# Gate rows, residual rows and split operands moved inside the product stages of a three-layer diffusion transformer

## Chip, cores and metric

One core of a Trainium2 chip. The metric is the device time of one launch in microseconds. All arithmetic is fp32; large products are made of fp32r parts (see below).

## The reference, cut to what matters

Width 1024, 512 latent tokens (`x`) and 256 context tokens (`ctx`). A first block (pooling, differential attention and a bidirectional RWKV scan, merged, then a routed expert layer) works on the latent rows alone. Two further layers work on both: one with hyena and mLSTM mixers, one with latent attention, each with a convolutional FFN (inner width 2816). Every residual step has the same form:

```
mod   = silu(c) @ w_ada + b_ada                    # six chunks of 1024, one is the gate of this step
x     = x + gate * (mixed @ w_out)                 # gate: one value a column, the same for all tokens
...
return rmsnorm(x, final_norm)                      # x * rsqrt(mean(x*x) + 1e-6) * final_norm
```

There are six such steps: output projection and experts in the first block, output projection and FFN down in each of the two layers; those of the middle layer also update `ctx`, with gates of its own. All but the experts' step go through `project_add`, five calls.

## The kernel before, in words

The program is a line of stages. `stage` (L46 to L66) opens a block in which each engine runs its own list; at its end all engines meet, and GpSimd clears the stage's semaphores. Work of one stage never overlaps work of the next, except for one weight tile that is asked for at the end of a product stage (`bring_ahead`) and lands behind the barrier.

`products` (L169) is the stage that does all large products. Weights of 256 columns come by DMA from SyncE (SP) into a landing buffer of 8 KB a partition. With `split=True`, ScalarE copies the landed tile into a leading part rounded to fp32r, in two halves (L276), VectorE subtracts to get the rest (L284), and TensorE adds three products, rest times leading, leading times rest, leading times leading (L340). The next step's load waits until the present tile is parted. Operands must lie in two parts as well. Results go from PSUM through `evac`, on ScalarE or VectorE. `side` are small products for later modulations, woven between. `pooled` is work for GpSimd in the same block. Without `split` (the branch products, `w_br`) three weight slots are filled from the stage's start on, and no weight is brought ahead.

`modulation_tiles` leave each modulation in `m.mod` with the column on the partitions. The residual step needs it along the free axis, the same on all 128 partitions. `gate_rows` (L444) makes that in a stage of its own: VectorE spreads a chunk to 128 equal columns (`wide`, L463), TensorE multiplies with the identity (L457, eight matmuls a row), VectorE copies from PSUM (L466). `halves` (L107) is another stage that splits the whole operand (L115 ScalarE, L121 VectorE). `project_add` (L1808) then runs the products with an evacuation of two instructions a tile: times the gate (L1821), added to the row (L1822). The order at the end of the first block is: gates' products, branch products, `load` of x (L825, a stage with one DMA and a wait), `gate_rows`, `halves`, `project_add`. The second block begins with a `load` of ctx. The FFN of the middle layer splits its operand inside the product stage, per k (`whole=`), so it has no `halves`, and nor has the last layer, whose FFN up writes both parts.

The end: `load` of the final gain, `head_norms` (L615 on: square, sum, root, reciprocal, times root, times gain, each VectorE pass over 128x4096), and a stage with one store of 2 MB (L2242).

`normed` (L475) makes row norms ahead of the products: ScalarE squares with a sum (L543) into a scratch tile, then the root (L537).

Of the kernel before, what the change touches and what calls it, by code (L numbers as in the profile page):

```python
# [168 lines left out]
def products(nc, m, jobs, xT, evac, evac_on, banks=4, kt=KD, wslots=WSLOTS, beside=None, width=512, split=False, k_chunks=1, side=(), pooled=None, whole=None):  # L169
# [18 lines left out]
    with ExitStack() as ctx:  # L188
# [8 lines left out]
        with stage(nc, w_landed=wslots, rounded=1, parted=1, made=1, read=1, chain=1, aux=1, side_landed=SIDE_SLOTS, side_made=1, side_copied=1, side_turned=1, side_read=1, spread=1, own_rounded=1, own_parted=1) as (  # L197
# [24 lines left out]
            def _(sp):  # L222
# [4 lines left out]

                ahead = 2 if split else wslots
# [22 lines left out]
                if split and m.ahead_next < len(m.ahead_of):  # L251
                    sp.wait_ge(parted_sem, 2 * len(steps))
                    bring_ahead(m, sp)

# [13 lines left out]
            def round_weights(act, s):  # L268
                if whole is not None and steps[s][0] == 0:
                    round_operands(act, s)  # L270
                if s >= 2:
                    act.wait_ge(made_sem, ends[s - 1])
                act.wait_ge(landed[s % wslots], landed_before[s % wslots] + sum(landings[s % wslots:s + 1:wslots]))
                n = steps[s][2]
                for k0, k1 in k_halves(s):
                    nc.scalar.copy(leading[s % 2][:, k0:k1, 0:n], slots[s % wslots][:, k0:k1, 0:n]).then_inc(rounded_sem, 1)  # L276

            def part_weights(dve, s):
                if whole is not None and steps[s][0] == 0:
                    part_operands(dve, s)  # L280
                n = steps[s][2]
                for q, (k0, k1) in enumerate(k_halves(s)):
                    dve.wait_ge(rounded_sem, 2 * s + q + 1)
                    nc.vector.tensor_tensor(rest[s % 2][:, k0:k1, 0:n], slots[s % wslots][:, k0:k1, 0:n], leading[s % 2][:, k0:k1, 0:n].bitcast(F32), ALU.subtract).then_inc(parted_sem, 1)  # L284

# [23 lines left out]
            def _(pe):  # L309
# [134 lines left out]
def gate_rows(nc, m, ctx, i, chunk, n, more=None):  # L444

    (rows,) = buffers(nc, ctx, gate_rows=[n, D])
    total = n + (more is not None)
    of = [(chunk, j) for j in range(n)] + ([(more[0], 0)] if more else [])
    with ExitStack() as own:
        (wide,) = buffers(nc, own, wide=[total, KD, P])  # L450
        with stage(nc, widened=1, made=1) as (block, widened_sem, made_sem):
            @block.tensor
            def _(pe):
                for j in range(total):
                    pe.wait_ge(widened_sem, j + 1)
                    for f in range(KD):
                        mm = nc.tensor.matmul(m.ps[:, 2 * j + f // 4, (f % 4) * P:(f % 4 + 1) * P], wide[:, j, f, :], m.ident, start=True, stop=True)  # L457
                    mm.then_inc(made_sem, 1)

            @block.vector  # L460
            def _(dve):
                for j, (c, kind) in enumerate(of):
                    nc.vector.tensor_copy(wide[:, j, :, :], bc(m.mod[:, i, KD * c:KD * (c + 1), kind:kind + 1], P)).then_inc(widened_sem, 1)  # L463
                for j in range(n):
                    dve.wait_ge(made_sem, j + 1)
                    nc.vector.tensor_copy(rows[:, j, :], m.ps[:, 2 * j:2 * j + 2, :].rearrange("p a b -> p (a b)"))  # L466
                if more:
                    dve.wait_ge(made_sem, total)
                    for h in range(2):
                        R = slice(64 * h, 64 * (h + 1))  # L470
                        nc.vector.tensor_copy(more[1][R, :], m.ps[R, 2 * n + h, :])
    return rows


def normed(nc, m, tiles, hT, affine, loads=None):  # L475
# [8 lines left out]
    with ExitStack() as ctx:  # L484
        b = Memory()
        b.sq, b.diag, b.whole, b.ss, b.root, b.rstd, b.gain = buffers(nc, ctx, sq=[2, D], diag=[n, P], whole=[4 if parts else 1, 512], ss=[n], root=[n], rstd=[n], gain=[len(kinds), KD])
# [435 lines left out]

# [2065 lines left out]
```

## Time and profile before

| | |
|---|---|
| median of 3 runs | 4127.73 us (4127.23, 4127.73, 4131.23) |
| span of the profiled execution | 4129.6 us; the page gives no time around it |
| TensorE matmul busy | 3568.4 us, 86% |
| VectorE / ScalarE / GpSimd busy | 1697.6 / 908.8 / 31.9 us |
| mean granted TensorE clock | 0.923 |
| DMA | 483.19 MB, 117 GB/s on average |

The span runs from the first to the last instruction. Busy times of different engines overlap and can't be added. The granted clock is 1.0 at 2.4 GHz and 0.5 at 1.2 GHz. The page's chain of waits holds only the last norm and store, since each stage ends at a barrier; to see what a stage costs, one reads the time between first instructions of neighbouring stages.

### The profile page before, as it was taken

How to read it: one execution, taken by the hardware profiler on the slowest of the kernel's cores; microseconds unless marked ns; L12 is line 12 of the kernel's file. 1: busy time of each engine (PE TensorE's matmuls, PEld its weight loads, DVE VectorE, ACT ScalarE, POOL GpSimd, SP SyncE). 2: the span in 40 equal slices, each digit the busy share in tenths (PEclk: the TensorE clock that was granted, in tenths of full speed). 3: DMA queues.
4: the chain of work that ended last, by engine and by line, in shares of the span. 5: the costliest groups of instructions: out<-in, count | busy, mean ns of one | idle time of the engine just before them, and what ended most of it. 6: DMA issues, size and time to landing. Idle time of an engine off the chain costs nothing. (4 is left out here: it accounts for less than half of the span.)

```text
span 4129.6 us, 71104 instructions
## 1 busy us (share of the span) xinstructions
PE 3568.4 (86%) x31286; PEld 2846.9 (69%) x31286; DVE 1697.6 (41%) x2906; ACT 908.8 (22%) x1502; POOL 31.9 (1%) x32
## 2 busy tenths in 40 slices
PE   5979997677997899995989976899989859979996
PEld 3858895655847655654746846888889856568886
DVE  3644544472123211113545256444452353245633
ACT  2135431041202111112011151211121212323221
POOL 0000000000000000000000000000000000000000
PEclk8979997888998899997999988999999989989998
DMA  6130004302344699993521100244422110013322
GB/s 225 57 129 4 4 4 166 123 1 94 92 143 161 253 408 410 412 412 122 174 81 56 52 2 31 65 124 115 121 75 64 43 36 25 1 52 93 97 74 80
DMA packets 274375, 483.19 MB, mean 117 GB/s; under 512 B 11947, under 2 KB 190668, under 8 KB 265397
## 3 DMA queue, kind: packets, MB, share of 16 engines
q1 hardware_dynamic: 267252, 453.97, 31.5%
q0 software_dynamic: 1728, 16.78, 1.1%
q10 hardware_dynamic: 5120, 8.39, 0.6%
q8 instruction: 220, 3.60, 0.4%
q14 instruction: 55, 0.44, 0.0%
HBM read 449.74 MB, written 29.36 MB: 116 GB/s over the span
## 5 line engine op out<-in xcount | busy, mean ns | idle before, releaser
L340 PE MATMUL banks<-leading,w_rest 128*128 128x512 f32 (+2 forms) x1920 | 698.9, 364 | 58.4 <-DVE w_rest L284 58.4
L340 PE MATMUL banks<-rest,w_leading 128*128 128x512 f32 (+2 forms) x1920 | 690.1, 359 | 0.0
L340 PE MATMUL banks<-leading,w_leading 128*128 128x512 f32 (+2 forms) x1920 | 688.9, 359 | 0.0
L284 DVE TENSOR_TENSOR w_rest<-land,w_leading 128x1024 fp32r<-128x1024 f32 (+2 forms) x328 | 306.9, 977 | 433.8 <-ACT w_leading L276 433.8
L276 ACT CAST w_leading<-land 128x1024 fp32r<-128x1024 f32 (+2 forms) x328 | 262.9, 849 | 875.4 <-DMA land<-in_w_in 303.0
L340 PEld LDWEIGHTS banks<-leading,w_rest 128*128 128x128 f32 (+1 forms) x1920 | 363.8, 189 | 128.8 <-DVE w_rest L284 46.0
L340 PE MATMUL banks<-w_rest,leading 128*128 128x256 f32 (+3 forms) x1332 | 394.4, 296 | 56.8 <-DVE w_rest L284 56.8
L340 PEld LDWEIGHTS banks<-leading,w_leading 128*128 128x128 f32 (+1 forms) x1920 | 364.1, 190 | 59.1
L340 PEld LDWEIGHTS banks<-rest,w_leading 128*128 128x128 f32 (+1 forms) x1920 | 364.0, 190 | 56.6
L340 PE MATMUL banks<-w_leading,rest 128*128 128x256 f32 (+3 forms) x1332 | 389.8, 293 | 0.0
L340 PE MATMUL banks<-w_leading,leading 128*128 128x256 f32 (+3 forms) x1332 | 389.4, 292 | 0.0
L340 PEld LDWEIGHTS banks<-w_rest,leading 128*128 128x128 f32 x1332 | 261.6, 196 | 66.3 <-DVE w_rest L284 53.0
L340 PEld LDWEIGHTS banks<-w_leading,rest 128*128 128x128 f32 x1332 | 261.4, 196 | 1.4
L340 PEld LDWEIGHTS banks<-w_leading,leading 128*128 128x128 f32 x1332 | 261.1, 196 | 1.4
L340 PE MATMUL banks<-w_rest,first_up_leading 128*128 128x256 f32 x528 | 150.4, 285 | 8.6 <-DVE w_rest L284 8.6
L340 PE MATMUL banks<-w_leading,first_up_rest 128*128 128x256 f32 x528 | 150.2, 284 | 0.0
L340 PE MATMUL banks<-w_leading,first_up_leading 128*128 128x256 f32 x528 | 150.2, 284 | 0.0
L2041 PE MATMUL banks<-wd,hT 128*64 128x512 f32 x512 | 125.3, 634 | 26.9 <-ACT hT L2065 26.9
L2098 DVE TENSOR_TENSOR y<-banks,expert_gate 128x512 f32<-128x512 f32 x32 | 22.1, 692 | 276.2 <-PE banks L2041 276.2
L2026 PE MATMUL banks<-wg,xT 128*64 128x256 f32 x1024 | 117.6, 383 | 1.2 <-ACT xT L2053 1.2
L1821 DVE TENSOR_TENSOR t<-banks,gate_rows 128x256 f32<-128x256 f32 x96 | 40.6, 423 | 185.6 <-PE banks L340 185.3
L2026 PE MATMUL banks<-wu,xT 128*64 128x256 f32 x1024 | 115.9, 379 | 0.0
(550 smaller groups left out, 5220.5 us busy)
## 6 DMA issues: line engine op xcount, KB each, us to landing
wg<-in_w_exp_gate SPq DMA_DIRECT2D x32, 2048.0 KB, 12.7
wu<-in_w_exp_up SPq DMA_DIRECT2D x32, 2048.0 KB, 14.8
wd<-in_w_exp_down SPq DMA_DIRECT2D x32, 2048.0 KB, 11.9
ws<-in_ada_w SPq DMA_DIRECT2D x96, 512.0 KB, 3.8
land<-in_w_in SPq DMA_DIRECT2D x41, 1024.0 KB, 5.4
land<-in_ffn_up SPq DMA_DIRECT2D x44, 512.0 KB, 5.4
land<-in_ffn_up SPq DMA_DIRECT2D x88, 256.0 KB, 3.3
land<-in_ffn_down SPq DMA_DIRECT2D x24, 768.0 KB, 4.9
```

Source lines behind the costliest of these rows:

```text
L276: nc.scalar.copy(leading[s % 2][:, k0:k1, 0:n], slots[s % wslots][:, k0:k1, 0:n]).then_inc(rounded_sem, 1)
L284: nc.vector.tensor_tensor(rest[s % 2][:, k0:k1, 0:n], slots[s % wslots][:, k0:k1, 0:n], leading[s % 2][:, k0:k1, 0:n].bitcast(F32), ALU.su ...
L340: mm = nc.tensor.matmul(bank_of(r, kind, at), lhsT, rhs, start=(k == 0 and q == 0), stop=(k == kt - 1 and q == len(each) - 1))
L1821: chain(nc.vector.tensor_tensor(b.t[:, turn[0], 0:width], out, g[:, c], ALU.mult))
L2026: mm = nc.tensor.matmul(m.ps[SLOTS * c:SLOTS * (c + 1), bank, half(u)], b.xT[:, k, S], w[u][:, k, half(c)], start=(k == 0), stop=(k == KD ...
L2041: mm = nc.tensor.matmul(m.ps[SLOTS * n:SLOTS * (n + 1), 5 + u, :], b.hT[:, j, SLOTS * c:SLOTS * (c + 1)], wd[u][:, k, n * 512:(n + 1) * 51 ...
L2098: nc.vector.tensor_tensor(y[u][:, :], m.ps[:, 5 + u, :], e.gate[:, :], ALU.mult).then_inc(y_read_sem, 1)
```

## The change

- Gate rows: no stage of their own. In three product stages that end well before the use, GpSimd's queue writes the gate chunks from `m.mod` to a DRAM buffer of eight rows, element by element (`keep_gate_rows`): two rows in the first block's gates' products, four in mLSTM's gates' products, two in the first FFN down. Each `project_add` has SP wait for the written rows and then load its one or two rows, spread to 128 partitions, at the head of its own stage (`bring_gate_rows`); VectorE waits for them before the first result.
- x is loaded at the head of the branch products, ctx and the experts' gate at the head of the first block's projection, the final gain at the head of the last FFN down. SP waits for them at the stage's end (`rows_landed`).
- In three projections the operand is split per token tile inside the product stage (`by_tile`): tile 0 ahead of the first weights, the others behind them; TensorE waits per tile.
- The last FFN down squares, on ScalarE, the columns that the round before has finished; `closing` squares the last 256 columns, adds the four sums, and scales and stores tile by tile.
- The experts' `normed` squares into PSUM banks instead of a scratch tile.

```diff
+                if early is not None:
+                    early(sp)
                 ahead = 2 if split else wslots
...
+                if late is not None:
+                    late(sp)
+            def round_tile(act, i):
+                x, hi, lo, shift = by_tile
+                nc.scalar.copy(hi[:, :, tile_columns(i)], x[:, :, tile_columns(i)]).then_inc(own_rounded_sem, 1)
+            def part_tile(dve, i):
+                x, hi, lo, shift = by_tile
+                dve.wait_ge(own_rounded_sem, i + 1)
+                nc.vector.tensor_tensor(lo[:, :, tile_columns(i)], x[:, :, tile_columns(i)], hi[:, :, tile_columns(i)].bitcast(F32), ALU.subtract).then_inc(own_parted_sem, 1)
...
+                if by_tile is not None and s == 0:
+                    round_tile(act, 0)
...
                 for k0, k1 in k_halves(s):
                     nc.scalar.copy(leading[s % 2][:, k0:k1, 0:n], slots[s % wslots][:, k0:k1, 0:n]).then_inc(rounded_sem, 1)
+                if by_tile is not None and s == 0:
+                    for i in range(1, len(steps[0][3])):
+                        round_tile(act, i)
...
+                            if by_tile is not None and j == 0 and k == 0:
+                                pe.wait_ge(own_parted_sem, i + 1)
...
-def gate_rows(nc, m, ctx, i, chunk, n, more=None):
...
+GATE_ROWS = ((0, 2, 0), (0, 5, 0), (1, 2, 0), (1, 2, 1), (1, 5, 0), (1, 5, 1), (2, 2, 0), (2, 5, 0))
+def keep_gate_rows(m, pool, i):
+    for row, (block, chunk, kind) in enumerate(GATE_ROWS):
+        if block == i:
+            pool.dma_start(m.gate_dram[row].rearrange("(f p) -> p f", p=P), m.mod[:, i, KD * chunk:KD * (chunk + 1), kind], allow_slow_non_contiguous=True).then_inc(m.gate_kept_sem, 16)
+            m.gates_kept += 16
+def bring_gate_rows(m, sp, i, chunk, rows):
+    sp.wait_ge(m.gate_kept_sem, m.gates_kept)
+    for kind in range(rows.shape[1]):
+        row = GATE_ROWS.index((i, chunk, kind))
+        sp.dma_start(rows[:, kind, :], m.gate_dram[row:row + 1, :].to_broadcast([P, D])).then_inc(m.gate_back_sem, 16)
+        m.gates_back += 16
...
-            load(nc, [(m.x, a["x"].rearrange("(t p) d -> p t d", p=P))])
-            gate = gate_rows(nc, m, mix, 0, 2, 1, more=(5, expert_gate))
-            with halves(nc, m.merged) as pair:
-                project_add(nc, m, a["w_out"], of_halves(pair), KD, [(t, m.x[:, t, :], gate[:, 0, :]) for t in range(NTL)], split=True, width=256)
+            def next_rows(sp):
+                row = GATE_ROWS.index((0, 5, 0))
+                for h in range(2):
+                    sp.dma_start(expert_gate[64 * h:64 * (h + 1), :], m.gate_dram[row:row + 1, 512 * h:512 * (h + 1)].to_broadcast([64, 512])).then_inc(m.rows_sem, 16)
+                sp.dma_start(m.xc[:, :, :], a["ctx_2"].rearrange("(t p) d -> p t d", p=P)).then_inc(m.rows_sem, 16)
+            hi, lo = two_parts(nc, mix, KD, LAT)
+            project_add(nc, m, a["w_out"], of_halves((hi, lo)), KD, [(t, m.x[:, t, :], 0) for t in range(NTL)], (0, 2, 1), split=True, width=256,
+                        by_tile=(m.merged, hi, lo, 0), early=next_rows, late=rows_landed(m))
...
+        def first_rows(sp):
+            sp.dma_start(m.x[:, :, :], a["x"].rearrange("(t p) d -> p t d", p=P)).then_inc(m.rows_sem, 16)
...
-        products(nc, m, jobs, lambda k, t0, tn, j: branch[j // 4][:, k, t0:t0 + tn], evac, "vector", kt=KB, width=256, side=modulation_tiles(m, a, 1, 0, 16))
+        products(nc, m, jobs, lambda k, t0, tn, j: branch[j // 4][:, k, t0:t0 + tn], evac, "vector", kt=KB, width=256, side=modulation_tiles(m, a, 1, 0, 16),
+                 early=first_rows, late=rows_landed(m))
...
+            if j == 0 and at[0] == tiles[0][0]:
+                nc.vector.wait_ge(m.gate_back_sem, m.gates_back)
...
+        def square(act, r, j, at, read_sem, aux_sem):
+            if r >= len(tiles):
+                before, (t, x, kind) = j - 1, tiles[r % len(tiles)]
+                act.wait_ge(read_sem, r - len(tiles) + 1)
+                nc.scalar.activation(squares[0][:, r % 2, 0:width], x[:, width * before:width * (before + 1)], ACT.Square, accum_out=squares[1][:, r % len(tiles), before:before + 1]).then_inc(aux_sem, 1)
...
+                for t in range(NTL):
+                    nc.scalar.activation(m.final_junk[:, t % 2, 0:256], m.x[:, t, last], ACT.Square, accum_out=m.final_ss[:, t, 3:4]).then_inc(squared_sem, 1)
+                act.wait_ge(summed_sem, 1)
+                nc.scalar.activation(b.root[:, :], b.sums[:, :], ACT.Sqrt).then_inc(rooted_sem, 1)
...
+                chain(nc.vector.tensor_reduce(b.sums[:, :], m.final_ss[:, :, :], AX, ALU.add))
+                nc.vector.tensor_scalar(b.sums[:, :], b.sums[:, :], 1.0 / D, EPS, ALU.mult, ALU.add).then_inc(summed_sem, 1)
+                chain(nc.vector.reciprocal(b.rstd[:, :], b.root[:, :]))
+                for t in range(NTL):
+                    nc.vector.scalar_tensor_tensor(m.x[:, t, :], m.x[:, t, :], b.rstd[:, t:t + 1], m.final_gain[:, :], ALU.mult, ALU.mult).then_inc(scaled_sem, 1)
...
+                for t in range(NTL):
+                    sp.wait_ge(scaled_sem, t + 1)
+                    sp.dma_start(a["out"][0][t * P:(t + 1) * P, :], m.x[:, t, :]).then_inc(stored_sem, 16)
```

## Rows read from the trace of the kernel before

**Rows 1.** The page, first section: busy us, share of the span, instructions.

```profile
PE 3568.4 (86%) x31286; PEld 2846.9 (69%) x31286; DVE 1697.6 (41%) x2906; ACT 908.8 (22%) x1502; POOL 31.9 (1%) x32
```

**Rows 2.** Stretches: length, busy us (instructions) of five engines, clock, DMA share, GB/s.

```profile
1008.00:1137.00 129.00, 128.31 (x566) 105.92 (x564) 25.96 (x22) 36.70 (x47) 0.00 (x0) 1.00 0.31 92
1140.70:1143.00 2.30, 2.27 (x4) 1.03 (x5) 0.00 (x0) 0.00 (x0) 0.00 (x0) 0.64 0.92 290
1265.00:1271.00 6.00, 6.00 (x28) 6.00 (x29) 1.52 (x3) 0.00 (x0) 0.00 (x0) 0.50 0.55 175
2296.00:2385.00 89.00, 86.22 (x576) 73.44 (x576) 9.81 (x10) 19.45 (x35) 0.00 (x0) 0.97 0.16 49
```

**Rows 3.** Timeline, first projection: start, length, engine, line, operation [idle before <-releaser].

```profile
1248.00 1.30 DVE L463 COPY wide<-mod 128x1024 f32<-128x1024 f32 x2 [8.39 <-PEq L57]
...
1263.68 2.36 DVE L284 TENSOR_TENSOR w_rest<-land,w_leading 128x1024 fp32r<-128x1024 f32 x2 [1.37 <-ACT w_leading L276]
...
1256.76 4.26 ACT L115 CAST leading<-merged 128x512 fp32r<-128x512 f32 x8 [119.81 <-PEq L57]
1262.61 1.99 ACT L276 CAST w_leading<-land 128x1024 fp32r<-128x1024 f32 x2 [1.59 <-PEq L57]
...
1264.96 0.58 PE L340 MATMUL banks<-w_rest,leading 128*128 128x256 f32 x1 [9.91 <-DVE w_rest L284]
```

**Rows 4.** DMA issues by line: count, KB each, median us from issue to landing.

```profile
x_rows<-in_x SPq DMA_DIRECT2D x1, 2048.0 KB, 7.7
...
final_gain<-in_rows SPq DMA_DIRECT2D x1, 512.0 KB, 3.6
```

**Rows 5.** Timeline, start of the branch products, SP and TensorE.

```profile
1137.20 0.37 SPq L239 DMA_DIRECT2D w<-in_w_br  x1
...
1140.73 2.32 PE L340 MATMUL banks<-brT,w 128*128 128x512 f32 x3 [4.41 <-DMA w<-in_w_br]
```

**Rows 6.** Timeline, VectorE behind the load of ctx.

```profile
1921.96 0.24 DVE L572 SCALAR_TENSOR_TENSOR gain<-mod,cols 128x8 f32<-128x8 f32 x2 [6.47 <-PEq L57]
```

**Rows 7.** Timeline, projection of hyena and mLSTM, VectorE and ScalarE.

```profile
2524.34 1.29 DVE L463 COPY wide<-mod 128x1024 f32<-128x1024 f32 x2 [0.88 <-PEq L57]
...
2541.25 1.99 ACT L276 CAST w_leading<-land 128x1024 fp32r<-128x1024 f32 x2 [2.23 <-PEq L57]
```

**Rows 8.** Timeline, the other three projections, VectorE and ScalarE.

```profile
3055.92 1.29 DVE L463 COPY wide<-mod 128x1024 f32<-128x1024 f32 x2 [0.32 <-PEq L57]
...
3062.05 4.50 ACT L259 CAST first_up_leading<-fT 128x768 fp32r<-128x768 f32 x6 [12.89 <-PEq L57]
...
3623.58 0.69 DVE L463 COPY wide<-mod 128x1024 f32<-128x1024 f32 x1 [0.32 <-PEq L57]
...
3633.77 1.99 ACT L276 CAST w_leading<-land 128x1024 fp32r<-128x1024 f32 x2 [1.59 <-PEq L57]
...
3961.23 0.69 DVE L463 COPY wide<-mod 128x1024 f32<-128x1024 f32 x1 [1.05 <-PEq L57]
...
3967.29 1.56 ACT L276 CAST w_leading<-land 128x768 fp32r<-128x768 f32 x2 [8.11 <-PEq L57]
```

**Rows 9.** Timeline, the end: last add of VectorE, SP's store.

```profile
4098.91 0.42 DVE L1822 TENSOR_TENSOR x_rows<-x_rows,t 128x256 f32<-128x256 f32 x1
...
4122.63 0.38 SPq L2242 DMA_DIRECT2D out<-x_rows  x1
```

**Rows 10.** Timeline, a row norm on ScalarE and a scaling on VectorE.

```profile
1924.02 1.04 ACT L543 ACTIVATE sq<-x_rows 128x1024 f32<-128x1024 f32 x1
...
1925.17 1.28 ACT L537 ACT_TABLE_LOAD   x1
1926.47 0.20 ACT L537 ACTIVATE root<-ss 128x2 f32<-128x2 f32 x1
...
1901.67 1.28 DVE L2121 SCALAR_TENSOR_TENSOR x_rows<-r,gate_of,x_rows 128x1024 f32<-128x1024 f32 x1 [9.57 <-DMA r<-expert_rows,place_of]
```

**Rows 11.** Groups of GpSimd: busy us, mean ns of one, idle before.

```profile
L2112 POOL DMA_INDIRECT r<-expert_rows,place_of x8 | 10.2, 1269 | 1246.5 <-issue 1246.5
```

More of the change, by code:

```diff
@@ L166, in bring_ahead, with products @@
     m.ahead_next += 1
-def products(nc, m, jobs, xT, evac, evac_on, banks=4, kt=KD, wslots=WSLOTS, beside=None, width=512, split=False, k_chunks=1, side=(), pooled=None, whole=None):
+def products(nc, m, jobs, xT, evac, evac_on, banks=4, kt=KD, wslots=WSLOTS, beside=None, width=512, split=False, k_chunks=1, side=(), pooled=None, whole=None, by_tile=None, early=None, late=None):
     size = -(-kt // k_chunks)
@@ L284, in part_weights @@
                     nc.vector.tensor_tensor(rest[s % 2][:, k0:k1, 0:n], slots[s % wslots][:, k0:k1, 0:n], leading[s % 2][:, k0:k1, 0:n].bitcast(F32), ALU.subtract).then_inc(parted_sem, 1)
+                if by_tile is not None and s == 0:
+                    for i in range(1, len(steps[0][3])):
+                        part_tile(dve, i)
             def bank_of(r, kind, at):
@@ L441, in modulation_tiles @@
     return [(w[:, f * P:(f + 4) * P], m.cond[:, i, :, :], m.mod[:, i, f:f + 4, :], bias[:, f:f + 4]) for f in range(first, end, 4)]
-def gate_rows(nc, m, ctx, i, chunk, n, more=None):
[L446 to L472, printed above, removed]
@@ L479, in normed @@
+def normed(nc, m, tiles, hT, affine, loads=None, squares=None):
     parts = hT if isinstance(hT, list) else None
@@ L485, in normed @@
         b = Memory()
-        b.sq, b.diag, b.whole, b.ss, b.root, b.rstd, b.gain = buffers(nc, ctx, sq=[2, D], diag=[n, P], whole=[4 if parts else 1, 512], ss=[n], root=[n], rstd=[n], gain=[len(kinds), KD])
+        b.diag, b.ss, b.root, b.rstd, b.gain = buffers(nc, ctx, diag=[n, P], ss=[n], root=[n], rstd=[n], gain=[len(kinds), KD])
+        b.sq = squares
+        if squares is None:
+            (b.sq,) = buffers(nc, ctx, sq=[2, D])
+        if parts:
+            (b.whole,) = buffers(nc, ctx, whole=[4, 512])
         def by_scalar(u):
@@ L1810, in project_add @@
+def project_add(nc, m, w, xT, kt, tiles, gate_of, wslots=3, width=512, split=False, banks=4, k_chunks=1, whole=None, by_tile=None, early=None, late=None, squares=None, pooled=None):
     jobs = [(w[:, c:c + width], width, [("N", t, width) for t, _, _ in tiles]) for c in range(0, D, width)]
-    by_tile = {t: (x, g) for t, x, g in tiles}
+    row_of = {t: (x, kind) for t, x, kind in tiles}
+    block, chunk, kinds = gate_of
     with ExitStack() as ctx:
         b = Memory()
-        (b.t,) = buffers(nc, ctx, t=[2, width])
+        b.t, b.gate = buffers(nc, ctx, t=[2, width], gate=[kinds, D])
@@ L1827, in first_highest @@
+        products(nc, m, jobs, xT, evac, "vector", kt=kt, wslots=wslots, width=width, split=split, banks=banks, k_chunks=k_chunks, whole=whole,
+                 by_tile=by_tile, pooled=pooled, early=rows_first, late=late, beside=None if squares is None else square)
 def first_highest(nc, chain, values, top, found, iota, work, hot):
@@ L2199, in second_block @@
                     mlstm(nc, m, a)
-                    tiles = adds(c1, 2)
-                    with halves(nc, m.mixT) as pair:
-                        project_add(nc, m, a["w_out_0"], of_halves(pair), KD, tiles, split=True, width=256)
+                    hi, lo = two_parts(nc, c1, KD, TOK)
+                    project_add(nc, m, a["w_out_0"], of_halves((hi, lo)), KD, adds, (1, 2, n), split=True, width=256, by_tile=(m.mixT, hi, lo, 0))
                 else:
@@ L2225, in second_block, with last_gain @@
                 if layer:
-                    project_add(nc, m, a["ffn_down_1"], of_halves(m.fT, first), KF, adds(c1, 5), width=256, split=True, banks=8, k_chunks=4)
+                    def last_gain(sp):
+                        sp.dma_start(m.final_gain[:, :], a["rows"][:, 6 * HD:6 * HD + D].to_broadcast([P, D])).then_inc(m.rows_sem, 16)
+                        m.rows_count += 16
+                    project_add(nc, m, a["ffn_down_1"], of_halves(m.fT, first), KF, adds, (2, 5, n), width=256, split=True, banks=8, k_chunks=4,
+                                early=last_gain, late=rows_landed(m), squares=(m.final_junk, m.final_ss))
                 else:
```

85 lines of the change are left out of this document (56 added, 29 removed).

## Prediction

> **What bounds the kernel now.** The page's first section first [rows 1]: TensorE is busy for 3568.4 of 4129.6 us, so 561 us of the span have no matmul, and whatever the change gains must come out of those. The stretches of busy time by engine next [rows 2]: inside a long product stage TensorE works 128.3 of 129 us at granted clock 1.00, so there is nothing to take there. The idle lies between stages. The timeline of each engine around the output projection of the first block [rows 3] shows the chain: VectorE idles 8.39 us before the first `wide` copy (the load of x, 2 MB, alone in its stage), then come the gate rows, then the split of `merged` into two parts (L115, L121), then the first weight half, and only then a matmul, after 9.91 us without one. The page's chain of waits covers only the last norm, so I read each stretch as the time from the first instruction of a removed stage to the first instruction of the stage behind it. The whole program is a line of stages with a barrier between, so time taken out of a stage that has no long matmul work comes off the end one for one. The sum is made against the profiled span, 4129.6 us. That is 1.9 us above the median of the three runs (4127.73); the page gives no other time for that execution, so I take the difference and subtract it from the median.
>
> **The change part by part.**
>
> *Stage for x, gate rows and split, first block.* The `wide` copy starts at 1248.00 after 8.39 us idle. Of it some 0.35 remain as the step from one stage to the next (two such steps are 0.32 in [rows 8]), so the load frees 8.0. From 1248.00 to 1262.61, where ScalarE rounds the first weights, gate rows and split together take 14.6 [rows 3]. Together 22.65. Added: the first token tile is rounded and parted ahead of the weights. It has 8x128 = 1024 elements, as a weight half has; two halves take 1.99 on ScalarE and 2.36 on VectorE, so one tile is 1.0 and 1.18. ScalarE is done with it at 1.0, VectorE at 2.2, the first weight half is parted at 3.4 instead of 2.24: matmuls start 1.15 later in the stage. Tiles 1 to 3 are parted at 5.8, 7.0 and 8.2 after the stage's start, while TensorE takes 24 matmuls a tile: at the slow clock's 213 ns (28 matmuls in the 6.0 us of [rows 2]) that is 5.1 us, so tile 1 is wanted at 8.6. Hidden by 2.8 us. The weights of step 1 are asked for 1.2 us later and behind 1.75 MB of gate rows, gate of the experts and ctx; step 0 lasts over 13 us and the load, rounding and parting want some 10 to 11, so this too lies beside matmuls. Net of this part: 21.5.
>
> *The load of x, moved.* SP now issues it at the head of the branch products, ahead of the first `w` of that stage. That stage's weights are not brought ahead: `w` is issued at 1137.20 and the first matmul, 4.41 us idle, starts at 1140.73, 3.5 after [rows 5]. On one queue the weights stand behind 2 MB. A 2 MB load landed in 7.7 us, 0.5 MB in 3.6 [rows 4], so 2.5 MB take 7.7 + 4.1/1.5 x 0.5 = 9.0, and the first matmul comes at +9.0 instead of +3.5: **5.4 given back**. If the weights do not queue behind x it is 0; if the whole of x and of what is issued with it had to land first it is up to 7.7. I take 5.4. The Trainium skill says the same of the mechanism in "DMA: Bandwidth & Descriptors", section "Queues, rings and completion order": one issuing engine has one ring on each DMA engine and its descriptors are consumed in order; the row above does not show an order yet, and without the rule the part would be 21.5 instead of 16.1. First block: 21.5 - 5.4 = **16.1**.
>
> *ctx, second block.* VectorE idles 6.47 before L572 [rows 6], 0.35 remain: **6.1**. Its 1 MB now lands beside the first block's projection.
>
> *Projection of hyena and mLSTM.* From 2524.34 to 2541.25 [rows 7], 16.9, less 1.15 for the first tile: **15.8**. Six tiles, the last parted at 10.6 after the stage's start, wanted at over 20.
>
> *The other three projections* [rows 8]. First FFN down: 3055.92 to 3062.05, **6.1**, gate rows only. Latent attention: 3623.58 to 3633.77, 10.2 less 1.15, **9.0**. Second FFN down: 3961.23 to 3967.29, **6.1**.
>
> *The gate rows by DMA.* Eight rows are written by GpSimd's queue, 1024 elements of 4 bytes each, two in the gates' products (129 us), four in mLSTM's (89 us), two in the first FFN down, with GpSimd at 0.00 busy in the first two [rows 2]. No row shows such a transfer. From below its issue costs GpSimd next to nothing; from above, an indirect load of 128 rows took 1.27 to issue [rows 11], which for 1024 elements is 10.2, four of them 41 us, under the 89. Both are covered, cost 0. Reading a row back to 128 partitions is the form of final_gain's load, 3.6 us [rows 4], against a first use over 8 us into the stage: 0. The broken transfers may hold up weights, but those are asked for a step ahead, and the 12 steps of the gates' products share 129 us, 10.8 each. Bounds of the part: 0 to 8 us.
>
> *The end.* Before: last add ends at 4099.33 (4098.91 + 0.42), then load, norm and store, this issued at 4122.63, span 4129.6 [rows 9]: 30.3 from last add to end. After: step 0.35; four squares of 256 columns. A square of 1024 takes 1.04 [rows 10]; a quarter with its fixed part I put at 0.4, between 0.26 and 1.04, so 1.6. The table load is 1.28 and starts right behind the squares, since the wait belongs to the root behind it (in [rows 10] it starts 0.11 after the square); the root follows 0.02 after it, 0.2, and the reciprocal 0.2. Four scalings of 128x1024 at 1.28, each of which scales by root and gain in one pass, 5.2. Sum 9.0. Each store of 512 KB leaves behind its own tile; the last lands in some 3.6 and 0.4 pass to the end of the span: 13.0 + 0.1. Gain **17.1** (16 to 18).
> Here the Trainium skill speaks against the change: "ScalarE: Activation LUTs", section "What ACT_TABLE_LOAD costs", has a drain of about 1.38 us beside the load, 2.66 together, and the load now stands on the path. By that the end gains 15.7 and the time is 1.4 later. In the trace load and root together leave no room for a drain behind the load (1925.17 + 1.28, root at 1926.47), so I go by the row.
>
> *Squares beside the last products* are twelve on ScalarE, which is busy for 22% of the span [rows 1], each of columns added a whole step before: 0. *Squares into PSUM* in the experts' norm: four, no row with such a target, -0.2 to +0.5 in all, taken 0. *Clock:* before each of the five calls of `project_add` the engine has idled 3.4 to 12 us, and starts at the low level: 28 matmuls in 6.0 us at 0.50 in the first [rows 2]. Afterwards the gap is still about 5 us, and 4.41 us [rows 5] were enough for granted clock 0.64 over the 2.3 us behind it [rows 2]. So I let the slow stretch stay, though it may be shorter. Its lengths here differ by 2 us, at half speed 1 us for each of five: +-3.
>
> Sum: 16.1 + 6.1 + 15.8 + 6.1 + 9.0 + 6.1 + 17.1 = **76.3**, and 4127.7 - 76.3 = **4051.4**.
>
> **Rivals.**
> 1. *x does not hold the branch weights back.* For it: the DMA share is low in these stretches. Against: all are issued by SP. Gain 81.7, time 4046.
> 2. *Given back in the stages that take over.* The 4-byte writes stall weight loads by the upper 8 us, step 1 of the first projection comes late behind 1.75 MB (up to 4), the slow clock lasts longer (3). Gain 61 to 70, time 4058 to 4066. For it: no row of such writes. Against: the slack of a whole step.
> 3. *Slower: GpSimd is the bound of the mLSTM gates' stage.* It must issue four of the rows between two barriers. The stage covers 89 us for 4096 elements, 22 ns an element; at 40 ns it lasts 165, all 76 us are gone, and beyond that the kernel is slower (at 60 ns 246 us, so 4127.7 - 76 + 157 = 4208). The dearest issue in the trace is 10 ns for each of 128 descriptors, so it would have to be four times that.
> 4. *The change does less than it says:* the gate rows are asked for and not there when the first result is ready. SP's wait for the written rows stands ahead of its weight loads, so that a late write holds everything; with writes issued 100 us and more before it, this has the same condition as 3, one stage later, and costs 10 to 20: 4062 to 4072.
>
> **How the numbers follow.** Forecast 0.62, rival 1 0.13, rival 2 0.15, rival 3 0.03, rival 4 0.05, something not seen 0.02. From 4051.4 with +-3 of clock, +-1 of the end and the bounds for x (5.4 back to 0, or up to 7.7) the own range is 4044 to 4057; rival 2's upper part stretches it to 4062. Range 4043 to 4062. About 0.2% (8.3 us) can be told from no change; that is reached unless 68 us are lost: faster 0.95, same 0.02, slower 0.03.
>
> **What would show it.** Between the last add of the branches and the first matmul of the projection under 6 us, no load stage, no `wide`. The first matmul of the branch products 9 us after SP's first issue instead of 3.5. First matmul of the three tile-wise projections 3.5 us after the stage's start, and none waiting for a tile later. GpSimd's issues done inside their stages. The last scaling 9 us behind the last add's stage, the end 13 behind the last add. Wrong: a stage that ends on GpSimd, a matmul idle behind `w_rest` in the middle of a projection, a root later than 0.1 us after its table load.

## The result and the profile after

| | before | after |
|---|---|---|
| median of 4 runs each, one chip | 4128.52 us (4127.23 to 4131.23) | 4073.99 us (4071.62 to 4076.78) |
| ratio, 95% interval | | 0.9865 (0.9852 to 0.9878) |
| span of the profiled execution | 4129.6 us | 4074.7 us |
| mean granted TensorE clock | 0.923 | 0.927 |

The kernel is 54.5 us faster by the medians, 54.9 by the spans. The forecast was 76.3, so 21.4 us of it are missing by the spans, and 4074 lies outside the range of 4043 to 4062. The direction was right and most terms held; one of them failed and is most of what is missing. The same kernel on another chip (run 7 below) took 4065.8 us, 60.1 less than the kernel before there, and lies outside the range too.

To see where, I cut both spans at the same points of the program: the first instruction of a stage, or the end of its last evacuation. Lengths in us:

| stretch | before | after | gained | forecast |
|---|---|---|---|---|
| to the first block's gates' products | 1000.7 | 999.7 | 1.0 | 0 |
| gates' products (two rows written beside) | 136.2 | 144.0 | **-7.8** | 0 |
| to the first branch result | 9.2 | 16.4 | **-7.2** | -5.4 |
| rest of the branches | 93.4 | 93.4 | 0 | 0 |
| to the experts' norm (first projection) | 75.6 | 53.3 | 22.3 | 21.5 |
| experts | 600.3 | 604.0 | -3.7 | 0 |
| to the second block's norm (ctx) | 6.4 | 1.0 | 5.4 | 6.1 |
| norm and hyena | 373.6 | 374.7 | -1.1 | 0 |
| mLSTM's gates' products (four rows beside) | 89.3 | 98.2 | **-8.9** | 0 |
| mLSTM | 138.7 | 138.8 | -0.1 | 0 |
| second projection | 92.5 | 76.3 | 16.2 | 15.8 |
| first FFN up | 439.6 | 439.5 | 0.2 | 0 |
| first FFN down (two rows beside) | 206.9 | 200.5 | 6.4 | 6.1 |
| latent attention | 360.8 | 360.5 | 0.3 | 0 |
| third projection | 62.1 | 53.9 | 8.2 | 9.0 |
| last FFN, up and down | 414.0 | 408.0 | 6.0 | 6.1 |
| last add to end | 30.3 | 12.4 | 17.9 | 17.1 |

Three stretches that were to be free or cheap are clearly longer, the bold ones. In the two stages of gates' products the weights of step 1 come late. The timeline after, GpSimd's issues of the written rows:

```profile
1000.62 1.83 POOL L485 DMA_DIRECT2D gate_rows<-mod  x2 [349.43 <-issue]
...
2288.16 3.63 POOL L485 DMA_DIRECT2D gate_rows<-mod  x4 [383.53 <-issue]
...
3041.47 1.76 POOL L485 DMA_DIRECT2D gate_rows<-mod  x2 [749.69 <-issue]
```

and ScalarE in the gates' products, where it waits for landed weights (the same stage of before follows, [rows 2] has its busy times):

```profile
999.69 1.99 ACT L299 CAST w_leading<-land 128x1024 fp32r<-128x1024 f32 x2 [31.48 <-PEq L57]
1018.05 1.99 ACT L299 CAST w_leading<-land 128x1024 fp32r<-128x1024 f32 x2 [16.37 <-DMA land<-in_w_in]
1027.20 2.00 ACT L299 CAST w_leading<-land 128x1024 fp32r<-128x1024 f32 x2 [4.76 <-DMA land<-in_w_in]
```

```profile
1000.71 1.99 ACT L276 CAST w_leading<-land 128x1024 fp32r<-128x1024 f32 x2 [31.83 <-PEq L57]
1011.03 2.00 ACT L276 CAST w_leading<-land 128x1024 fp32r<-128x1024 f32 x2 [8.34 <-DMA land<-in_w_in]
```

From the stage's start to the second rounding it is 18.4 us instead of 10.3. In mLSTM's gates' products, with four rows, it is 24.6 instead of 13.2 (after, then before):

```profile
2286.59 1.99 ACT L299 CAST w_leading<-land 128x1024 fp32r<-128x1024 f32 x2 [33.02 <-PEq L57]
2311.22 1.99 ACT L299 CAST w_leading<-land 128x1024 fp32r<-128x1024 f32 x2 [11.47 <-DMA land<-in_w_in]
```

```profile
2308.73 2.00 ACT L276 CAST w_leading<-land 128x1024 fp32r<-128x1024 f32 x2
```

What the first of these two stages waits for is in the DMA view of 1001 to 1019 us: busy share in tenths and GB/s of 40 slices, the queues, and the time from issue to landing.

```profile
DMA  0054540000000234759358674379448999620000
GB/s 0 0 5 4 5 4 0 0 0 0 0 0 0 43 55 80 32 30 30 9 23 27 25 25 18 18 59 46 50 105 253 357 371 369 216 98 30 0 0 0
...
q1 hardware_dynamic: 1040, 1.05, 37.1%
q0 software_dynamic: 64, 0.01, 5.2%
...
land<-in_w_in SPq DMA_DIRECT2D x1, 1024.0 KB, 14.9
gate_rows<-mod POOLq DMA_DIRECT2D x2, 4.0 KB, 10.7
```

For some 7 us the DMA engines show 20 to 90% busy and move 9 to 80 GB/s; only then, after the two written rows have landed, does the rate go to 350, and 1 MB of weights takes 14.9 us. The weights' own packets took 37.1% of 18 us, 6.7 us of each engine; in the kernel before, the same 1 MB landed in 6.8 us and its packets took 3.5 us of each engine.

**The first projection** after, VectorE, ScalarE and TensorE, answers to [rows 3]:

```profile
1253.90 1.05 ACT L268 CAST leading<-merged 128x1024 fp32r<-128x1024 f32 x1 [110.16 <-PEq L57]
1254.85 1.99 ACT L299 CAST w_leading<-land 128x1024 fp32r<-128x1024 f32 x2
1254.98 1.23 DVE L274 TENSOR_TENSOR rest<-merged,leading 128x1024 fp32r<-128x1024 f32 x1 [1.37 <-ACT leading L268]
1256.12 2.35 DVE L312 TENSOR_TENSOR w_rest<-land,w_leading 128x1024 fp32r<-128x1024 f32 x2
1257.39 0.58 PE L373 MATMUL banks<-w_rest,leading 128*128 128x256 f32 x1 [5.20 <-DVE w_rest L312]
1258.39 3.49 DVE L274 TENSOR_TENSOR rest<-merged,leading 128x1024 fp32r<-128x1024 f32 x3
1265.74 2.00 ACT L299 CAST w_leading<-land 128x1024 fp32r<-128x1024 f32 x2 [6.06 <-DMA land<-in_w_out]
```

No load stage and no `wide`; the matmul starts 3.5 us after the stage's first instruction and 5.2 us after the one before it, and tiles 1 to 3 are parted by 1261.9. The stretches of it (columns as in [rows 2]) have clock 0.50 at first and 1.00 from 1262 on, 4.6 us behind the first matmul; before, it was still 0.50 up to 1271, 6.0 us behind it [rows 2, 3]. Ahead of this matmul TensorE had idled 5.2 us, and 9.9 in the kernel before. Half of those 1.4 to 1.8 us is about the 0.8 by which this projection gained more than forecast.

```profile
1258.00:1260.00 2.00, 2.00 (x11) 2.00 (x11) 2.00 (x3) 1.68 (x2) 0.00 (x0) 0.50 0.98 331
1260.00:1262.00 2.00, 2.00 (x12) 2.00 (x12) 1.88 (x2) 0.00 (x0) 0.00 (x0) 0.57 1.04 383
1262.00:1264.00 2.00, 2.00 (x19) 2.00 (x18) 0.85 (x2) 0.00 (x0) 0.00 (x0) 1.00 0.97 316
```

**The experts' stretch** was to cost nothing and is 3.7 us longer. The two groups of 64 matmuls at its head, in the norm and in the router, after and then before:

```profile
1313.81 10.24 PE L640 MATMUL banks<-diag,x_rows 128*128 128x128 f32 x64 [8.18 <-DVE diag L612]
1325.17 12.55 PE L1931 MATMUL banks<-w,hT 128*128 128x36 f32 x64 [1.12 <-PEq L57]
```

```profile
1322.12 9.08 PE L611 MATMUL banks<-diag,x_rows 128*128 128x128 f32 x64 [8.17 <-DVE diag L583]
1332.32 10.59 PE L1864 MATMUL banks<-w,hT 128*128 128x36 f32 x64 [1.12 <-PEq L57]
```

They are 3.1 us longer. The granted clock is 0.50 in the first 5.0 us of the first group and 0.56 over the second; before, it was 0.65 and 0.67. From the first expert matmul to the end of the stretch it is 535.1 us after and 535.2 before.

**The start of the branches** after, SP and TensorE, answers to [rows 5]; in the third fence TensorE there before, its whole first group of eight:

```profile
1143.99 0.37 SPq L1838 DMA_DIRECT2D x_rows<-in_x  x1
1144.41 0.50 SPq L241 DMA_DIRECT2D w<-in_w_br  x1
```

```profile
1153.54 6.55 PE L373 MATMUL banks<-brT,w 128*128 128x512 f32 x8 [10.44 <-DMA w<-in_w_br]
```

```profile
1140.73 5.37 PE L340 MATMUL banks<-brT,w 128*128 128x512 f32 x8 [4.41 <-DMA w<-in_w_br]
```

**The end** after, ScalarE, VectorE and SP, answers to [rows 9, 10]:

```profile
4064.30 1.28 ACT L2322 ACT_TABLE_LOAD   x1
4065.60 0.21 ACT L2322 ACTIVATE root<-sums 128x4 f32<-128x4 f32 x1
```

```profile
4061.86 0.42 DVE L1878 TENSOR_TENSOR x_rows<-x_rows,t 128x256 f32<-128x256 f32 x1
...
4066.05 4.87 DVE L2333 SCALAR_TENSOR_TENSOR x_rows<-x_rows,rstd,final_gain 128x1024 f32<-128x1024 f32 x4
```

### The profile page after: what moved, and what is told of

It is laid out like the page before. It is cut to its first block and busy times, and to the rows that moved or that the text cites. A ratio compares the mean times of both kernels' runs of the same rounds, so it can differ in the third digit from the quotient of the medians.

```text
span 4074.7 us, 70734 instructions
## 1 busy us (share of the span) xinstructions
PE 3555.5 (87%) x31158; PEld 2833.6 (70%) x31158; DVE 1669.7 (41%) x2880; ACT 914.4 (22%) x1524; POOL 37.5 (1%) x40
## 5 line engine op out<-in xcount | busy, mean ns | idle before, releaser
L373 PE MATMUL banks<-w_rest,leading 128*128 128x256 f32 (+3 forms) x1332 | 396.6, 298 | 53.1 <-DVE w_rest L312 53.1
L1877 DVE TENSOR_TENSOR t<-banks,gate 128x256 f32<-128x256 f32 x96 | 40.7, 423 | 174.3 <-PE banks L373 174.0
```

What stands on the lines that cost most here:

```text
L373: mm = nc.tensor.matmul(bank_of(r, kind, at), lhsT, rhs, start=(k == 0 and q == 0), stop=(k == kt - 1 and q == len(each) - 1))
L1877: chain(nc.vector.tensor_tensor(b.t[:, turn[0], 0:width], out, b.gate[:, kind, c], ALU.mult))
```

## The experiments

The theories. **A**: the rows written element by element hold the DMA engines, so weights asked for meanwhile land late; its cost is per row and depends on what is wanted at that time. **C**: SP's queue is served in order, so the branch weights stand behind x. The expectations below name the rivals to each. "Changed kernel" is the one after. Every run is compared with the kernel before on its own chip (medians there 4126.1, 4126.0, 4126.0). The changed kernel itself was timed on the first chip and in run 7 only, and the ratio intervals of runs 1, 2, 4 and 5 overlap that of run 7 (0.984 to 0.9873). So what these runs say rests on the length of single stretches in one profile each, not on their totals.

**1. The writes spaced.** Each row waits on GpSimd until the first half of a later step's weights is rounded (steps are counted from 0): steps 2 and 3 in the gates' products, 1, 1, 2, 2 in mLSTM's, 4 and 5 in the first FFN down.

```diff
+    steps = {0: [2, 3], 1: [1, 1, 2, 2], 2: [4, 5]}[i]
...
+            pool.wait_ge(m.rounded_of, 2 * steps.pop(0) + 1)
```

> The changed kernel with one edit: GpSimd writes the gate rows later in the same stages, each only when a weight tile has just landed (gates' products: one in step 2, one in step 3; mLSTM gates: two in step 1, two in step 2; first FFN down: steps 4 and 5). Theory A (a row written in 1024 single elements holds all DMA engines some 5 us, and that stood ahead of step 1's weights): both stalls go, gates' products back from 144.3 to 136.5 us, mLSTM gates from 98.5 to 89.6, the time to 4057 (4055 to 4060). Rival B (the stages lose the time however the writes lie, by GpSimd's work or by traffic on the same memory): 4074, the stall only moves.

Measured 4061.03 us (4060.67 to 4064.14), ratio 0.9843 (0.9826 to 0.9859). mLSTM's gates are back at 89.2, the gates' products at 143.5 are not. ScalarE there, around the first spaced write, issued at 1022.92:

```profile
1021.59 2.00 ACT L299 CAST w_leading<-land 128x1024 fp32r<-128x1024 f32 x2 [2.00 <-DMA land<-in_w_in]
1038.15 2.00 ACT L299 CAST w_leading<-land 128x1024 fp32r<-128x1024 f32 x2 [7.68 <-DMA land<-in_w_in]
```

From one rounding to the next it is 9.1 us (1012.53 to 1021.59) without a write and 16.6 with one, where TensorE works some 10.7 us a step (128.31 us in twelve, [rows 2]): with one row beside it a load is already late. The two loads that stood beside one row landed 13.0 and 13.4 us after their issue, their neighbours in 5.2 to 5.5. mLSTM's steps are 17 us and hide two rows each. So the stall goes where there is slack, as A has it, and the half of my expectation that took one row per step to be free in both stages was wrong.

**2. The same rows in pieces of 64 bytes** (gate of both kinds, eight chunks, per partition, one run of 64 bytes; the buffer twice as large and the rows in another order, so the gates that are read back are not the reference's).

```diff
-            pool.dma_start(m.gate_dram[row].rearrange("(f p) -> p f", p=P), m.mod[:, i, KD * chunk:KD * (chunk + 1), kind], ...)
+            pool.dma_start(m.gate_dram[row].rearrange("(p f) -> p f", p=P), m.mod[:, i, KD * chunk:KD * (chunk + 1), :].rearrange("p f j -> p (f j)"))
```

> The changed kernel with each of the eight row writes as 128 pieces of 64 bytes (a partition's 8 columns of both kinds) instead of 1024 pieces of 4 bytes, at the same place; the gate values then stand in another order, so the output is another one. Theory A: a row lands in 2 to 3 us instead of 5 each behind another, stages back to 137 and 90, time 4058. Rival B, where it is the place of a GpSimd-issued write ahead of the weights or its issue that costs: 4074, unchanged.

Measured 4055.03 us (4052.65 to 4056.58), ratio 0.983 (0.9813 to 0.9846). Gates' products 136.2 and mLSTM's 89.0, both as before the change. The DMA view from 997 to 1008 us:

```profile
q1 hardware_dynamic: 1040, 1.05, 31.7%
q0 software_dynamic: 64, 0.02, 1.0%
...
land<-in_w_in SPq DMA_DIRECT2D x1, 1024.0 KB, 5.4
gate_rows<-mod POOLq DMA_DIRECT2D x2, 8.0 KB, 1.7
```

Twice the bytes in an eighth of the pieces land in 1.7 us instead of 10.7, and the weights in 5.4 instead of 14.9; their packets take 31.7% of 11 us, 3.5 us of an engine instead of 6.7. So the pieces are the cause, not the queue, the issue on GpSimd or the bytes. Whether it is their number (1024 against 128) or their size (4 bytes against 64) this run can't tell, since both were changed together.

**3. Every row written twice**, the second time to another buffer.

```diff
+            pool.dma_start(m.gate_dram_2[row].rearrange("(f p) -> p f", p=P), m.mod[:, i, KD * chunk:KD * (chunk + 1), kind], ...)
```

> The changed kernel with every gate row written twice (the second copy to another buffer). Theory A: 5.1 us a row more ahead of step 1's weights: gates' products 144.3 + 10 = 154.5, mLSTM gates 98.5 + 20 = 119, and first FFN down loses some 5 to 10 that its operand split no longer hides: time 4109 to 4114. Rival B: GpSimd's issue of 0.9 us a row more, 4074 to 4080.

Measured 4110.05 us (4104.11 to 4112.09), ratio 0.9957 (0.994 to 0.9974). The load of step 1 in the gates' products landed 23.7 us after its issue. Gates' products 152.7 (+8.7 for two more rows), mLSTM's gates 119.4 (+21.2 for four), first FFN down 208.0 (+7.5 for two): 4.4, 5.3 and 3.8 us a row, so the FFN down, which hid two rows, pays for four. Against the changed kernel's second profile (run 7) the same three are 5.3, 5.9 and 3.8.

**4. x behind the branch weights.** SP issues x after the three first weight tiles and the two side tiles.

```diff
+                    if s == 2 and behind is not None:
+                        behind(sp)
...
-                 early=first_rows, late=rows_landed(m))
+                 behind=first_rows, late=rows_landed(m))
```

> The changed kernel with the load of x issued behind the first three branch weights and two side weights instead of ahead of them. Theory C (SP's transfers are served in the order of issue, and 2 MB ahead of the first weights cost 7.2 us): first matmul 3.5 us after the stage's start, branch products back from 109.6 to 102.4, time 4067. Rival D (x shares the bandwidth with the weights wherever it stands, or something else in the stage is slower): 4070 to 4074.

Measured 4062.84 us (4060.09 to 4067.45), ratio 0.9848 (0.9832 to 0.9864). First branch result after 9.3 us instead of 16.4, all of the 7.2 lost (in run 7's profile of the changed kernel it is 15.9). TensorE there:

```profile
1149.33 5.37 PE L375 MATMUL banks<-brT,w 128*128 128x512 f32 x8 [4.56 <-DMA w<-in_w_br]
```

The rest of the branches and the first projection are as in the changed kernel (93.4, 53.1): x has 90 us to land.

**5. x on another queue**, issued by ScalarE at the same point.

```diff
+                if beside_act is not None:
+                    beside_act(nc.scalar)
...
-                 early=first_rows, late=rows_landed(m))
+                 beside_act=first_rows, late=rows_landed(m))
```

> Changed kernel, but the 2 MB of x at the start of the branch products are issued from ScalarE's queue instead of SP's, still at the stage's start; the branch weights stay on SP's. Theory C (one issuing engine's transfers are served in order, so the weights stood behind x): the weights only share the bandwidth with x, 0.5 MB at half of the 400 GB/s seen there take 2.5 us plus the landing's fixed part, and the first branch result comes 11 to 12 us after the last gate instead of 16.4; total 5 us under the changed kernel, 4066 to 4067 on a chip where that takes 4071.6. Rival D (the DMA engines are full and serve in order of arrival, whatever the queue): still 16 us, total 4071 to 4072.

Measured 4062.09 us (4058.55 to 4062.94), ratio 0.9845 (0.983 to 0.986); first branch result after 12.5 us. TensorE:

```profile
1143.94 5.61 PE L373 MATMUL banks<-brT,w 128*128 128x512 f32 x8 [7.51 <-DMA w<-in_w_br]
```

Its idle time is 7.5 us, between the 4.6 of x behind and the 10.4 of x ahead on the same queue. The weights, issued at 1137.32, came 6.6 us after their issue, between the 3.7 of run 4 and the 9.1 of the changed kernel. So x beside them costs some 3 us, whatever the queue, and x ahead of them on the same queue another 3 to 4. The second part is C's, but not shown by this run alone: ScalarE issued x at 1137.35, 0.03 us behind the weights, where SP had issued it 0.42 us ahead of them. The queue and the order of issue were changed together.

**6. The split in a stage of its own again**, in the three projections.

```diff
-            hi, lo = two_parts(nc, mix, KD, LAT)
-            project_add(... by_tile=(m.merged, hi, lo, 0), early=next_rows, late=rows_landed(m))
+            with halves(nc, m.merged) as pair:
+                project_add(... early=next_rows, late=rows_landed(m))
```

> Changed kernel, but the three projections split their operand again in a stage of its own ahead of the products (as before), not per token tile inside. My step of the sum: the stages took 5.85, 8.19 and 5.85 us, less 1.15 each for the first tile, so this kernel is 16.4 us slower than the changed one: 4088 where that takes 4071.6, with the three projection stretches 58.0, 83.3 and 58.6 us instead of 53.3, 76.3 and 53.9. Rival (tile by tile hands part of it back later, in late tiles or in a longer slow-clock stretch): it is only 8 to 12 us slower, 4080 to 4084.

Measured 4083.74 us (4082.9 to 4087.72), ratio 0.9896 (0.9881 to 0.9912). The three projections take 58.6, 83.2 and 58.5 us, against 53.3, 76.3 and 53.9: 5.3 + 6.9 + 4.6 = 16.8, forecast 16.4. Inside the projections nothing is given back. Behind the first one something is: from the experts' norm to the first expert matmul this run takes 65.4 us, as before the change (65.2), and the changed kernel 68.9, in run 7 67.9. TensorE's two groups there are back at 8.99 and 10.69 us. So the rival's longer slow stretch exists and takes 2.5 to 3.5 us of the 16.8. The total does not decide between the two: 4083.74 lies in the range that I had given the rival, but only because I took the changed kernel to be 4071.6 there. Against run 7, behind the start of the gates' products, the spans differ by 14.8. This run's gates' products (140.2) and mLSTM's gates (95.0) were shorter than in the first profile of the changed kernel, which led to the next run.

**7. The changed kernel once more**, on the chip of the next run.

> The changed kernel unchanged, beside the next one. Two of the runs before this one, in which nothing of the written rows was changed, had gates' products of 140.2 us and mLSTM's gates of 95.0, against 144.0 and 98.2 in the first profile of the changed kernel. If the cost of the element-wise writes differs from execution to execution or from chip to chip by that much, this profile shows 140 to 144 and 95 to 98 and a total between 4065 and 4074. Rival: 144 and 98 belong to this kernel's own layout and come back exactly, total 4071 to 4072 beside 4126 for the kernel before.

Measured 4065.84 us (4065.57 to 4068.16), before 4125.98 there, ratio 0.9857 (0.984 to 0.9873). Gates' products 142.0, mLSTM's gates 95.6, experts 601.6. The weights of step 1 landed 14.0 us after their issue. So the stall is there again, and 5 us smaller in the two stages together; the ratio's interval overlaps the first one's. The six profiles of kernels with unchanged writes range from 140.2 to 144.0 and from 95.0 to 98.2, so the stall of the two stages together from 9.7 to 16.7 us; the first profile is the largest. The experts' stretch over all profiles is 599.6 to 604.0.

**8. The old end.**

```diff
+    load(nc, [(m.final_gain, a["rows"][:, 6 * HD:6 * HD + D].to_broadcast([P, D]))])
+    head_norms(nc, m, [(m.x[:, :, :], m.final_gain[:, :])], D, EPS)
...
-    closing(nc, m, a)
```

> Changed kernel with the old ending: final gain loaded in a stage of its own, row norm over all rows on VectorE, one store. My step of the sum: 17.1 us lost; the stretch from last add to end read 30.3 us before and 12.4 after, so 17.9: this kernel ends 17 to 18 us later than the changed kernel beside it. Rival (the squares beside the last products cost those something): the last FFN down is shorter than 133.1 us by up to 1 us and the loss is smaller by that.

Measured 4088.54 us (4085.28 to 4092.7), 22.7 over the run beside it, where 17 to 18 were expected; the spans differ by 21.7. The end itself reads 30.9 instead of 12.4, 18.5. Another 5.4 of the spans' difference lie before 1004 us, in a part that the edit doesn't touch and that varies from 997 to 1006 between profiles, and between the two the run is 2.2 shorter. The last FFN down is 133.1 in both, so the twelve squares beside it cost nothing.

**9. The three repairs together**: the first block's rows written in the attention stage, which loads no weights; those of mLSTM's stage spaced as in 1; x as in 4.

```diff
-attention(nc, m, items, 2, HD ** -0.5, m.neg_lam[:, :])
+attention(nc, m, items, 2, HD ** -0.5, m.neg_lam[:, :], pooled=lambda pool: keep_gate_rows(m, pool, 0))
...
+    steps = [1, 1, 2, 2]
...
+            if i == 1:
+                pool.wait_ge(m.rounded_of, 2 * steps.pop(0) + 1)
```

> Changed kernel with three edits: the first block's two gate rows are written in the attention stage, which loads no weights; the second block's four rows in mLSTM's gates' products each wait for a weight step (steps 1, 1, 2, 2); x is issued behind the first three branch weights. Theories A and C together (element-wise writes hold up weights that are just then wanted; SP's queue is served in order): gates' products back to 136.2 from 144.0, first branch result 9.3 instead of 16.4, mLSTM's gates back to 89.2 from 98.2, so 23.9 us under the changed kernel: 4047 to 4049 where that takes 4071.6. Rival (the DMA time of the writes is paid wherever they stand): the start before the gates grows by about 8 us and the time is 4055 to 4057.

Measured 4048.78 us (4046.97 to 4051.13), ratio 0.9813 (0.98 to 0.9827). ScalarE in the gates' products:

```profile
1000.05 1.99 ACT L301 CAST w_leading<-land 128x1024 fp32r<-128x1024 f32 x2 [31.20 <-PEq L57]
1008.91 2.00 ACT L301 CAST w_leading<-land 128x1024 fp32r<-128x1024 f32 x2 [6.87 <-DMA land<-in_w_in]
```

Gates' products 135.4, first branch result 9.3, mLSTM's gates 89.0. Against run 7 these are 6.6 us each, 19.8 in all; mLSTM itself, which the edits don't touch, is 1.9 shorter (136.7). The rows, issued at 846.55, landed in 8.5 us, and the DMA engines show their packets for only 1 us of it. The attention stage lasts 81.3 us with the writes, as in the changed kernel and before: where nothing is loaded the writes are free. Rival fallen.

**10. The same, and the root's table loaded ahead**, by one small root beside the last products.

```diff
+                if r == len(tiles) + 2:
+                    nc.scalar.activation(m.final_early[:, :], squares[1][:, 0, 0:1], ACT.Sqrt)
```

> As the kernel before it in this list, and ScalarE takes one root of a single value a partition beside the last products, so that the root's table is loaded there and not in the closing stage. If the squares and copies that follow run with that table: the 1.28 us table load leaves the closing stage, its end 11.1 instead of 12.4 us after the last add, total 1.3 us under the kernel without it (4046 to 4047). Rival: the squares behind it bring their own table back, the load stays in the closing stage, no difference.

Measured 4047.61 us (4042.94 to 4048.81), ratio 0.9805 (0.9791 to 0.9818): not to be told from the ninth by its total. In the trace there is no table load in the closing stage, and from the last add to the end it is 11.5 us instead of 12.4. It saves 0.9 and not 1.28, because the root now waits 0.44 us for VectorE's sum, which had lain beside the load:

```profile
4037.55 0.21 ACT L2335 ACTIVATE root<-sums 128x4 f32<-128x4 f32 x1 [0.44 <-DVE sums L2342]
```

## Why the prediction was wrong, point by point

- **The step that failed: "Both are covered, cost 0", on the gate rows by DMA.** I asked whether GpSimd could issue the pieces in time, and it can: 0.9 us a row, less than a tenth of my upper bound. I did not price what the pieces do to the DMA engines beside them; "asked for a step ahead" was taken as a slack of 10.8 us, but of that step load, rounding and parting take 9 (the roundings of run 1), so under 2 us were free. It cost 16.7 us in the first profile (7.8 and 8.9), 12.1 in the second, and 9.7 to 16.7 over all six with unchanged writes. My bound for the part, 8 us, was meant for both stages and was passed in every one. Runs 1, 2, 3 and 9 show it by moving, widening, doubling and removing it. Rival 2 named this mechanism with its upper end of 8 and a chance of 0.15: right in kind, too small in size. Of its other parts, the late step 1 of the first projection did not come (TensorE never idled over 0.25 us there behind its first matmul), and the longer slow clock came in another place (experts, below).
- **The load of x ahead of the branch weights: mechanism right, term too small**, 7.2 instead of 5.4. The row gives the parts: 0.4 for the issue behind x's, 9.1 from issue to matmul instead of 3.5, which is 5.6, and 1.2 because the first eight matmuls took 6.55 us instead of 5.37, at clock 0.50 for longer, after 10.4 us of idling instead of 4.4. I had counted the clock for the projections only. The Trainium skill's rule of order ("DMA: Bandwidth & Descriptors", "Queues, rings and completion order") agrees with the changed kernel and run 4: 9.1 us from issue to matmul behind x, 3.7 ahead of it. The same section of the Trainium skill says that an engine takes turns between rings a packet at a time; by that the branch weights on a queue of their own come earlier than behind x, with which run 5 agrees (6.6), and weights beside written rows should wait a packet's turn only. That section gives no price for a packet of 4-byte pieces, and here 1 MB beside two rows took 14.0 to 14.9 us instead of 5.4 to 6.8.
- **Stages taken out: right.** First projection 22.3 (21.5), second 16.2 (15.8), third 8.2 (9.0), the two FFN down 6.4 and 6.0 (6.1 each), ctx 5.4 (6.1). Later tiles were never waited for. In the first FFN down the two written rows cost nothing, since its weights have room there.
- **The end: 17.9 (17.1).** Scalings took 1.22 us each, not 1.28, and the last store landed in 2.9 us, not 3.6. The squares were 0.40, as estimated. For the root the row decided well: table load 4064.30 + 1.28, root at 4065.60, no room for the drain of 1.38 us that the Trainium skill has in "ScalarE: Activation LUTs", "What ACT_TABLE_LOAD costs". Here page and measurement differ, and the measurement counts.
- **Experts, 3.7 us: the clock, counted in the wrong place.** All of it lies ahead of the first expert matmul, 3.1 in the two groups of matmuls shown above. It is not the squares into PSUM, since run 6 has them too and takes 65.4 us to that matmul; with the tile-wise split it is 67.9 to 68.9 in nine profiles of ten, and 64.8 in run 1. I had put the clock at +-3 on the slow starts of the five projections, and said that the idle time ahead of them would shrink to about 5 us; it shrank to 5.2 to 8.3. Why the clock rises later behind the first projection is not shown. What lies behind the first expert matmul scatters by itself, 533.6 to 536.2. In mLSTM too the clock differs with nothing edited there: 138.7 us in seven profiles and 136.7 in five, all in one stage (some 94.3 at clock 0.90 to 0.91, 92.4 at 0.94); no run was aimed at that, and it stays open.
- **The range** was built from +-3 of clock and the bounds of x, with the unknown transfer at 8 for the whole kernel. An operation for which no row existed was given a bound that no row stood behind.
- **What stays open**: what inside the DMA engines holds the weights while 4-byte pieces are written. The records show the slow packets and the low rate, not the reason, and not why one execution pays 9.7 us for it and another 16.7.

## What to carry to other kernels

A DMA of 4-byte pieces is cheap to issue and dear beside it: count its pieces, not its bytes. Here 1024 of them made a 1 MB load beside them land some 8 us later (run 1), 2048 some 9 and 4096 some 18 (run 3). Put it in a stage that loads nothing, or in steps whose slack (step minus load, rounding and parting) is larger than that. A load that is moved to the head of a stage goes behind that stage's first weights on the queue, not ahead of them. And when a cost has no row, the question "who issues it" is not enough; ask what it shares.

## What the runs showed of the hardware that I had not expected

- One row of 1024 4-byte elements from 128 partitions to DRAM holds up other loads by 4 to 6 us where others are written beside it (run 3: 3.8 to 5.9 us a row) and a single load by some 8 us where it is alone (run 1: 13.0 and 13.4 instead of 5.2 to 5.5), though GpSimd issues it in 0.9 us; the same row in 64-byte pieces costs nothing that shows.
- While such rows were being written the engines showed 20 to 90% busy at 9 to 80 GB/s; the busy share alone would have passed for useful traffic. Two rows with nothing beside them took 8.5 us to land, and their packets 1 us of the engines (run 9).
- Where a stage was taken out ahead of the first projection, TensorE came back to clock 1.00 some 4.3 us after its first matmul instead of 6.1 us. In the second projection it took 3.9 us, and 4.0 before, so this gain is not to be counted on. And behind the first projection the clock stayed at 0.50 for longer than before, which handed 2.7 to 3.7 us back in nine profiles of ten.
